# Gate and up: the four weight differences of a block made by GpSimd instead of VectorE

## The reference

```
g = h @ w_gate                       # 2048 x 5632
c = conv_b + sum_j ext[:, j:j+L] * conv_w[j]      # 3 taps over g and its state
out = (silu(c) * (h @ w_up)) @ w_down
```

## Time and profile before

| what | value |
|---|---|
| median of 3 runs | 2773.61 us (2771.68 to 2773.92) |
| profiled execution, its span | 2774.62 us, 2772.5 us |
| PE busy | 2670.9 us (96%) |
| DVE busy | 1859.3 us (67%) |
| ACT busy | 1212.6 us (44%) |
| POOL busy | 0.8 us, 7 instructions |
| loads of w_gate, w_up: 88 each, 512 KB | 4.7 and 4.6 us from issue to landing |

### The profile page before, as it was taken

One profiled execution on the slowest core, in us unless ns is written; L12 is line 12 of the kernel. 1 busy time (PEld: TensorE's weight loads), 2 busy tenths in 40 slices (PEclk: granted clock), 3 DMA queues, 4 the chain that ended last, 5 costly groups with the idle time before them and its releaser, 6 DMA issues. The chain is left out here.

```text
span 2772.5 us, 51672 instructions
## 1 busy us (share of the span) xinstructions
PE 2670.9 (96%) x20527; PEld 2513.4 (91%) x20527; DVE 1859.3 (67%) x3000; ACT 1212.6 (44%) x1731; POOL 0.8 (0%) x7
## 2 busy tenths in 40 slices
PE   7999999999999997999999999999889999999998
PEld 7989889889888986999999999999778888899998
DVE  5676666666666466888888888888655555576444
ACT  6445545545545245444444444444422232244222
POOL 0000000000000000000000000000000000000000
PEclk9999999999999998999999999999999999999999
DMA  6343343344346353434434434344533333333332
GB/s 219 107 135 108 111 140 114 101 142 116 100 138 200 114 152 103 126 116 119 124 105 123 120 115 125 105 122 119 165 117 103 106 103 106 103 90 91 110 105 85
DMA packets 570809, 333.05 MB, mean 120 GB/s; under 512 B 18120, under 2 KB 545346, under 8 KB 570602
## 3 DMA queue, kind: packets, MB, share of 16 engines
q1 hardware_dynamic: 538298, 304.71, 37.2%
q10 hardware_dynamic: 32320, 25.68, 2.9%
HBM read 290.73 MB, written 39.77 MB: 119 GB/s over the span
## 5 line engine op out<-in xcount | busy, mean ns | idle before, releaser
L1095 PE MATMUL product<-act,w_hi 128*128 128x512 f32 x1504 | 618.1, 411 | 19.4 <-DVE w_lo L1828 12.6
L1314 ACT ACTIVATE w_hi<-w_raw 128x1024 fp32r<-128x1024 f32 (+1 forms) x322 | 330.1, 1026 | 621.5 <-PE product L1099 525.2
L1828 DVE TENSOR_TENSOR w_lo<-w_raw,w_hi 128x1024 fp32r<-128x1024 f32 (+1 forms) x322 | 380.9, 1183 | 292.8 <-ACT w_hi L1314 292.3
L1099 PE MATMUL product<-act,w_lo 128*128 128x264 f32 x1504 | 430.4, 286 | 0.0
L1096 PE MATMUL product<-act,w_hi 128*128 128x264 f32 x1504 | 427.0, 284 | 0.0
L1097 PE MATMUL product<-act,w_hi 128*128 128x264 f32 x1504 | 424.7, 282 | 0.0
L1098 PE MATMUL product<-act,w_lo 128*128 128x256 f32 x1504 | 422.9, 281 | 0.0
L1097 PEld LDWEIGHTS product<-act,w_hi 128*128 128x128 f32 x1504 | 283.2, 188 | 68.1
L1095 PEld LDWEIGHTS product<-act,w_hi 128*128 128x128 f32 x1504 | 285.3, 190 | 38.5 <-issue 20.6
L1096 PEld LDWEIGHTS product<-act,w_hi 128*128 128x128 f32 x1504 | 285.7, 190 | 0.9
L1099 PEld LDWEIGHTS product<-act,w_lo 128*128 128x128 f32 x1504 | 283.1, 188 | 0.0
(11 more groups left out here) (315 smaller groups left out, 6039.7 us busy)
## 6 DMA issues: line engine op xcount, KB each, us to landing
w_raw<-in_w_in SPq DMA_DIRECT2D x112, 512.0 KB, 3.9
w_more<-in_w_up SPq DMA_DIRECT2D x88, 512.0 KB, 4.6
w_raw<-in_w_gate SPq DMA_DIRECT2D x88, 512.0 KB, 4.7
w_raw<-in_w_down SPq DMA_DIRECT2D x64, 384.0 KB, 3.5
w_raw<-in_w_down SPq DMA_DIRECT2D x64, 320.0 KB, 3.2
w_raw<-in_w_out SPq DMA_DIRECT2D x32, 512.0 KB, 4.8
w_raw<-in_w_ple_gate SPq DMA_DIRECT2D x32, 384.0 KB, 3.3
u_scratch<-xT SPq DMA_DIRECT2D x44, 260.0 KB, 2.1
```

The costliest lines, as they stand in the source:

```text
L1095: pe.matmul(both, hi, x[:, k, 0:2 * TA], start=begin, stop=False)
L1099: mm = pe.matmul(far, lo, x[:, k, 2 * TA:TA + T], start=False, stop=end)
L1314: act.activation(w_hi[:, slot, 0:n, :], w_raw[:, slot, 0:n, :], ACT.Copy).then_inc(w_hi_ready, 1)
L1828: dve.tensor_tensor(flat(w_lo[:, slot, 0:n, :]), flat(w_raw[:, slot, 0:n, :]), flat(w_hi[:, slot, 0:n, :]).bitcast(F32), ALU.subtract).the ...
```

## The change

VectorE's program loses w_difference and its calls. GpSimd gets a loop over the 44 blocks with the same four subtractions. In addition to the waits that the differences had, difference 1 waits until w_low 0 of its block is done (w_lo_ready, since it writes over raw_gate[0], which w_low 0 reads), and difference 4 until w_low 1 is done. The loads, the casts and the products are unchanged and still wait for w_summed.

```diff
-                w_difference(0, 1)
-                w_difference(0, 2)
...
-                    if f > 0:
-                        w_difference(f, 3)
                     w_low(f, 2)
...
-                    w_difference(f, 4)
...
                         w_low(f + 1, 0)
-                        w_difference(f + 1, 1)
                     up_near(f)
-                    if f + 1 < FB:
-                        w_difference(f + 1, 2)
...
     @block.gpsimd
     def _(pool):
         def visit(what, arg):
+            if what == "ffn":
+                summed = flag("w_summed")
+                for f in range(FB):
+                    pool.wait_ge(flag("up_in0"), (f + 1) * 16)
+                    pool.wait_ge(w_lo_ready, prep(f, 0) + 1)
+                    pool.tensor_tensor(flat(raw_gate[0]), flat(raw_up[0]), flat(raw_gate[0]), ALU.subtract).then_inc(summed, 1)
+                    pool.wait_ge(flag("up_in1"), (f + 1) * 16)
+                    pool.wait_ge(summed, 4 * f + 1)
+                    pool.tensor_tensor(flat(w_two), flat(raw_up[1]), flat(raw_gate[0]), ALU.subtract).then_inc(summed, 1)
+                    pool.tensor_tensor(flat(raw_up[0]), flat(raw_up[1]), flat(raw_up[0]), ALU.subtract).then_inc(summed, 1)
+                    pool.wait_ge(w_lo_ready, prep(f, 1) + 1)
+                    pool.wait_ge(summed, 4 * f + 2)
+                    pool.tensor_tensor(flat(raw_gate[1]), flat(raw_gate[1]), flat(w_two), ALU.subtract).then_inc(summed, 1)
```

More of the change, by code:

```diff
@@ L2108, in operand @@
             t.then_inc(flag("act_lo_ready"), 1)
[L2110 to L2125, removed]
         def x_sums_of(it, apart=False):
```

## The result

The changed kernel takes 2869.68 us (median of 4 runs, 2865.15 to 2872.62), the one before 2773.7: a ratio of 1.0346, 95% interval 1.0328 to 1.0364. It is slower by 96 us; 2836 was forecast, in a range of 2771 to 2907. The profiled execution has a span of 2870.5 us, 98.0 more than before.

What follows compares the result with a forecast made beforehand. TensorE was taken to bound the gate and up stage, so relieving VectorE gains nothing there. Turns between GpSimd and VectorE add 43 to 82 us, middle 62: 2773.6 + 62 = 2836 us, range 2771 to 2907.

Steps and rivals of the forecast that it cites:

- No gain on VectorE's side: Gate and up blocks 1 to 43: removing the differences from VectorE is worth nothing, since TensorE does not wait there.
- the turns: GpSimd differences and VectorE instructions with two SBUF inputs go in turns, each for its whole length: 43 to 82 us; chance 0.60.
- the rival without turns: GpSimd's 8.8 us a block lie wholly beside VectorE and TensorE, the start gains 1.9 us: 2772 us; chance 0.23.
- GpSimd's subtraction: One 128x1024 difference on GpSimd, scaled from memsets: 2.2 us taken, bounds 0.95 and 2.6 us.
- The alternating order: Within a block, GpSimd differences and VectorE's w_lo strictly alternate, product 3 starts 1.0 us late: 43 x 1.0 = 43 us.
- D: Length of one GpSimd difference, taken as 2.2 us.
- Three in a row: GpSimd keeps its turn through difference 3, w_lo of product 1 waits, product 1 starts 1.9 us late: 43 x 1.9 = 82 us.
- "That does not change": Cast 1 on ScalarE waits 3.42 us for its gate weights behind a DMA; claimed to stay so after the change.
- Block 0 at nothing: Stage start: the 1.9 us gained are lost again where difference 1 stands before the x sums, net zero.
- The sum: Whole kernel: 2773.6 + 62 = 2836 us, 62 being the middle between 43 and 82 us.

Runs made afterwards that it cites:

- Experiments 1: Kernel before, plus four GpSimd subtractions of 128x1024 a block (blocks 1 to 40) whose results no engine waits for: 3051.68 us, ratio 1.1003.
- 2: Kernel before, plus four idle GpSimd memsets of 128x2048 a block, which write SBUF and read nothing: 2774.09 us, ratio 1.0002.
- 3: Kernel before, plus four idle GpSimd copies of 128x1024 a block, one SBUF input each: 2786.19 us, ratio 1.0049.
- 9: Kernel before with block 0's differences 1 and 2 later, and difference 1 of blocks 1 to 43 on GpSimd: 2772.35 us, ratio 0.9997 to the kernel before.
- Experiment 12: Changed kernel with raw_gate[1] of blocks 1 to 43 loaded by half, outputs not the reference's: 2844.16 us, ratio 1.0259 to the kernel before.
- Experiments 4: Changed kernel with difference 3 placed behind the wait for w_low 1 instead of ahead of it: 2839.65 us, ratio 1.0236 to the kernel before.
- experiment 5: Changed kernel with each difference as two GpSimd instructions of 128x512: 2843.34 us, ratio 1.0249 to the kernel before.

## Why the prediction was right

**No gain on VectorE's side, and the turns:** right. Experiments 1, 2, 3 and 9 show each by itself, and the rival without turns has fallen. The Trainium skill, page "SBUF — State Buffer", section "SBUF: two separate sides", says that a VectorE instruction with two SBUF inputs and a GpSimd instruction that reads SBUF exclude each other, each for its whole length; the runs agree, with 1.22 us for a w_lo beside memsets and up to 3.4 beside subtractions.

**GpSimd's subtraction:** 2.40 us, not 2.2, inside the bounds of 0.95 and 2.6. The estimate of 2.25 us, from the page "GPSIMD Engine Reference", section 3.1, of the Trainium skill, is 6% short.

**The alternating order:** its 1.0 us a block becomes 1.8 with four turns of 2.40, and 1.6 was measured (21.87 against 20.27). The turns came in the order that the sum has, and D was its term that was too small. But the sum let product 3 wait for lo 3 alone, which ends at 1521.92 in the block shown. What TensorE waited for is gate_far behind it, which ends at 1522.27; product 3 follows that. The forecast had no such term, so that its 1.8 comes near the 1.6 by offset in part. Experiment 12, which has only such blocks, confirms that they need no load in the explanation.

**Three in a row:** 1.9 us was forecast; 3 x 0.2 more for D makes 2.5, TensorE waited 2.2. The three blocks at full clock lost 2.6 (22.9 against 20.27), as this sum has it. The nine at the lower clock lost 4.1: the term that was missing is TensorE's clock, 1.5 us a block.

**"That does not change", of the load behind hi 1:** wrong. This was the step that failed. Before, lo 1 began 0.07 us behind product 0 (1510.21, 1510.14); in the two blocks shown of after it is 1.5 and 2.0 us behind (1513.91 and 1512.39, 1536.34 and 1534.36), because lo 6, held back with the rest of VectorE's chain, ends 4.8 us ahead of product 0 (1507.56) and no longer 5.8 (1504.30), and from the end of lo 6 to the start of hi 1, with the load between them, it is 5.3 and 5.8 us and no longer 4.8. ScalarE's cast 1 in these two blocks, where before it had 3.42 us of idle time ahead of it:

```profile
1512.82 1.06 ACT L1703 ACTIVATE w_hi<-w_raw 128x1024 fp32r<-128x1024 f32 x1 [5.04 <-DMA w_raw<-in_w_gate]
1535.25 1.06 ACT L1703 ACTIVATE w_hi<-w_raw 128x1024 fp32r<-128x1024 f32 x1 [5.59 <-DMA w_raw<-in_w_gate]
```

This chooses the order of the turns, which I had left open between two ends: 12 of 42 blocks are of the dear kind, 9 of them with the lower clock. Experiments 4 and 12 remove them in two ways, and take 30 and 26 us. Why the load itself varies no run shows.

**Block 0 at nothing:** wrong by 7 us (7.9 less the 0.85). The three sums are 0.42 us each, but each stood behind a difference of its own, where I had charged one, and x_sets stood behind a fourth. At that wait TensorE lost 5.7 us (11.99 against 6.29); the rest of the 7 comes between it and block 1, and was not followed.

**The sum.** The 98 us of the trace are 62.4 for the blocks at the alternating pace, 27.9 for the long ones, 7.9 for the start. The 62.4 are 42 x 1.6 = 67.2 less 4.8, mostly since four blocks of before were longer than 20.27 us. That this is the forecast's 62 is luck: the forecast had 43 us for alternating turns, too little by D and without gate_far, and added half the way from there to 82 for the other order, which the trace has in 12 blocks and which is counted in the 27.9. The 34 us that the forecast lacks are the other two terms, about (35.8).

## What to carry to other kernels

Before work goes from VectorE to GpSimd, mark in the timeline where VectorE runs instructions with two SBUF inputs: a GpSimd instruction that reads SBUF takes turns with each of them, for its whole length, and only gaps or instructions with a PSUM operand (0.42 us inside each of the 43 subtractions of experiment 9) cover it. Count what is held along every chain of waits that comes back in the next block, those through a DMA too, and for each wait of TensorE look at everything that stands in VectorE's queue ahead of it, and not only at the next w_lo. When the bounding engine was never waiting, as the earlier trace rows showed, such a move cannot win, however idle the other engine is.

## What the runs showed of the hardware

- A GpSimd fp32 subtraction of 128x1024 takes 2.40 us alone, of 128x512 1.3 us (groups of 1297 and 1305 ns in experiment 5), a memset of 128x2048 1.815 us. VectorE needs 1.22 us for the 128x1024.
- Turns go in the order of the requests: lo 1 and difference 3 kept to it in 42 of 42 blocks, down to leads of 0.02 and 0.08 us. The waiting stands inside the duration of the instruction, not in the idle time before it. A wait that no view names shows as a group whose mean grew (1.22 to 2.70 us for lo 2).
- Cutting an instruction in two does not halve what the other engine waits in all: 4.4 us a block in the mean against 4.8.
- After 2.2 to 2.4 us without work TensorE ran at the 1.2 GHz level for most of 3.7 us in 9 blocks, and at the 2.4 GHz level, without a fall, in 3 (waits of 2.20 to 2.24 us). What decides between them no run shows.
